# The norm behind w_o moved to scores and expert blocks, the residual turned raw, and decode's gelu put behind the next copy and split

## The reference

```python
x = x + mixed @ w_o
x = x + peer(rmsnorm(x, norm_ffn_g), peer_wq, keys1, keys2, u, v)

def rmsnorm(x, g):
    return x * rsqrt(mean(x * x, -1) + EPS) * g

def peer(x, wq, keys1, keys2, u, v):
    q  = (x @ wq)                       # 8 heads, 256 wide: two halves of 128
    s1 = q[..., :half] @ keys1.T        # scores; s2 likewise with keys2
    ...                                 # top 16 of each, top 16 of their sums, softmax -> gate
    z   = x @ u[expert]                 # inner products with the chosen experts
    act = gelu(z) * gate
    return act @ v[expert]
```

## Time and profile before

| | us |
|---|---|
| median of 3 runs | 2696.15 (2695.79 to 2697.1) |
| profiled execution | 2696.89 |
| its span | 2695.2 |
| PE busy | 2669.4 (99%) |
| DVE busy | 1835.3 (68%) |
| ACT busy | 1369.4 (51%) |
| POOL busy | 371.4 (14%) |

### The profile page before, as it was taken

One profiled execution on the slowest core, in us unless ns is written; L12 is line 12 of the kernel. 1 busy time (PEld: TensorE's weight loads), 2 busy tenths in 40 slices (PEclk: granted clock), 3 DMA queues, 4 the chain that ended last, 5 costly groups with the idle time before them and its releaser, 6 DMA issues.

```text
span 2695.2 us, 47112 instructions
## 1 busy us (share of the span) xinstructions
PE 2669.4 (99%) x14299; PEld 2298.4 (85%) x14299; DVE 1835.3 (68%) x2985; ACT 1369.4 (51%) x2066; POOL 371.4 (14%) x296
## 2 busy tenths in 40 slices
PE   8999999999999999999999999999999999999998
PEld 6888888898888998888888888888888888888887
DVE  6666665668987677489996777775565555555555
ACT  6454445555665444455455555554444444444444
POOL 0010000001011211011105555551000000000000
PEclk9999999999999999999999999999999999999999
DMA  7566555564554554655567777777976666666564
GB/s 257 189 216 213 181 199 177 177 219 159 172 176 156 167 168 157 195 201 186 195 201 212 202 202 203 201 204 218 305 240 217 217 217 219 212 220 216 200 241 156
DMA packets 204475, 543.26 MB, mean 202 GB/s; under 512 B 37504, under 2 KB 82816, under 8 KB 203392
## 3 DMA queue, kind: packets, MB, share of 16 engines
q1 hardware_dynamic: 148112, 486.74, 54.9%
q10 hardware_dynamic: 35568, 47.33, 5.0%
q0 software_dynamic: 20736, 8.46, 2.7%
HBM read 515.12 MB, written 27.33 MB: 201 GB/s over the span
## 4 chain that ended last, share of the span: by engine, by line
PE 94%; DVE 3%; ACT 1%; issue 1%; DMA 0%; SPq 0%; DVEq 0%; POOL 0%; ACTq 0%; POOLq 0%
PE bank L561 32%; PE bank L568 16%; PE bank L2693 8%; PE bank L2694 8%; PE bank L2695 8%; PE bank L601 4%; PE bank L603 4%; PE bank L602 4%; PE bank L2488 1%; DVE w_lo L504 1%; PE bank L527 1%; PE bank L528 1%; PE bank L529 1%; PE bank L2658 1%; PE bank L2465 0%
## 5 line engine op out<-in xcount | busy, mean ns | idle before, releaser
L504 DVE TENSOR_TENSOR w_lo<-raw,w_hi 128x1024 fp32r<-128x1024 f32 x902 | 1097.9, 1226 | 725.9 <-ACT w_hi L495 719.4
L495 ACT ACTIVATE w_hi<-raw 128x1024 fp32r<-128x1024 f32 x902 | 950.8, 1059 | 946.5 <-PE bank L568 363.1
L561 PE MATMUL bank<-act,w_hi 128*128 128x512 f32 x3840 | 975.2, 396 | 2.6 <-DVE cst L579 1.0
L561 PEld LDWEIGHTS bank<-act,w_hi 128*128 128x128 f32 x3840 | 692.0, 189 | 133.8 <-issue 6.4
L568 PEld LDWEIGHTS bank<-act,w_lo 128*128 128x128 f32 x3840 | 519.7, 190 | 33.1
L568 PE MATMUL bank<-act,w_lo 128*128 128x256 f32 x3840 | 535.6, 282 | 0.0
L2693 PE MATMUL bank<-w_hi,expert_act 128*128 128x512 f32 x1008 | 392.3, 389 | 0.1
L2694 PE MATMUL bank<-w_lo,expert_act 128*128 128x512 f32 x1008 | 392.2, 389 | 0.0
L2695 PE MATMUL bank<-w_hi,expert_act 128*128 128x512 f32 x1008 | 392.1, 389 | 0.0
L742 POOL DMA_INDIRECT g_kept<-slot_t x128 | 239.7, 1872 | 253.8 <-issue 170.4
L2693 PEld LDWEIGHTS bank<-w_hi,expert_act 128*128 128x128 f32 x1008 | 189.3, 188 | 39.6 <-DVE cst L579 0.5
(11 more groups left out here) (344 smaller groups left out, 2498.4 us busy)
## 6 DMA issues: line engine op xcount, KB each, us to landing
raw<-in_stream SPq DMA_DIRECT2D x902, 512.0 KB
z_kept<-cst ACTq DMA_DIRECT2D x112, 128.0 KB, 2.4
cst<-z_kept ACTq DMA_DIRECT2D x112, 128.0 KB, 3.9
g_kept<-zeros POOLq DMA_DIRECT2D x16, 512.0 KB
big<-in_ukv ACTq DMA_DIRECT2D x16, 512.0 KB, 4.6
big<-g_kept SPq DMA_DIRECT2D x16, 512.0 KB, 5.6
big<-in_rows ACTq DMA_DIRECT2D x3, 1024.0 KB, 5.8
big<-in_x SPq DMA_DIRECT2D x2, 1024.0 KB, 10.2
```

Source lines behind the costliest of these rows:

```text
L495: act.activation(w_hi[:, s, :], raw[:, s, :], ACT.Copy).then_inc(hi_ready, 1)
L504: dve.tensor_tensor(w_lo[:, s, :], raw[:, s, :], w_hi[:, s, :].bitcast(F32), ALU.subtract).then_inc(lo_ready, 1)
L561: pe.matmul(bank[:, :], w_hi[:, s, kk * P:(kk + 1) * P], act2[:, k, :, :].rearrange("p a n -> p (a n)"), start=(k == 0), stop=False)
```

## The change

It does four things.

1. X is turned without the norm. `turn_block` (eight transposes of a quarter of X's columns for one half of the tokens) is called with the raw X: three of the four blocks between units of w_o, the fourth between the two units of the first query pair. The hi and lo tiles come from the helpers that the first block uses, `keep_hi_tiles` and `keep_lo_tiles`. XN and its eight pieces are gone.
2. The factor 1/root (`rstd`, one number a token) is put on products instead. ACT's copy of the scores takes it as its scale, in two copies of 128 columns where there was one of 256. For the expert blocks, whose columns are tokens, DVE builds two diagonal tiles, PE multiplies them with ones to a row that is the same in all partitions, and ACT copies that row to `FFN_ROW`.
3. Each expert block is multiplied with `FFN_ROW` ahead of its gelu: the router's early blocks by POOL (`early_block`), the 16 decode blocks by POOL in a loop that stands ahead of the scatter, the 80 gates and 16 late blocks by DVE (`scale_rows`). ACT's gelu waits for `z_scaled` where it waited for the add.
4. In decode ACT's turn is now: split of unit 0, copy of block k, split of unit 1, and then gelu and store of block k-1.

```diff
+            def early_block(n, block):
+                z = Z_HALVES[:, n, 0:S]
+                pool.wait_ge(copied, block + 5)
+                step(pool.tensor_tensor(z, z, Z_HALVES[:, n, S:2 * S], ALU.add))
+                pool.wait_ge(row_kept, 2)
+                step.wait()
+                pool.tensor_tensor(z, z, FFN_ROW, ALU.mult).then_inc(pool_summed, 1)
...
+            with pool.Fori(0, PH) as i:
+                for n in range(2):
+                    wait_summed(pool, block_of("u_decode", i, 2, n))
+                    pool.tensor_tensor(GZ[:, n, :], GZ[:, n, :], FFN_ROW, ALU.mult).then_inc(z_scaled, 1)
             pool.wait_ge(picks_ready, 5)
...
+                        else:
+                            keep_hi_tiles(3, pa("ffn_gain"), act_hi, k // 4 - 1)
                         block_squares(added, base, k // 4 - 1)
...
-                if not t:
-                    ahead(split_hi, act, "w_o", 0, 8, 15, units=(0,))
-            act.wait_ge(rstd_ready, 7)
-            norm_second(2)
-            keep_ffn_hi(range(4))
-            norm_second(3)
-            keep_ffn_hi(range(4, 8))
+            ahead(split_hi, act, "w_o", 0, 8, 15, units=(0,))
+            keep_hi_tiles(3, pa("ffn_gain"), act_hi, 3)
             ahead(split_hi, act, "w_o", 0, 8, 15, units=(1,))
-            keep_ffn_hi(range(8, 16))
...
-                    act.activation(PS[:, a, :, :].rearrange("p t n -> p (t n)"), banks[4 + a][:, 0:S],
-                                   ACT.Copy).then_inc(ps_kept[a], 1)
+                    for t in range(TT):
+                        kept = act.activation(PS[:, a, t, :], banks[4 + a][:, t * P:(t + 1) * P], ACT.Copy,
+                                              scale=rstd[:, t:t + 1])
+                    kept.then_inc(ps_kept[a], 1)
...
+                if first:
+                    act.wait_ge(row_made, 2)
+                    act.activation(FFN_ROW, banks[6][:, 0:S], ACT.Copy).then_inc(row_kept, 1)
+                    act.wait_ge(rstd_ready, 7)
                 keep_scores(0)
...
                     ahead(split_hi, act, "u_decode", i, 2, n, units=(0,))
+                    act.wait_ge(unit_done, 2 * pair_of("u_decode", i, 2, n) + 2)
+                    act.wait_ge(z_saved[n], i * 16 + (16 * PH + 1))
+                    low_half(act, GZ[:, n, :], banks[2 + n])
+                    ahead(split_hi, act, "u_decode", i, 2, n, units=(1,))
                     if first and not n:
                         save_early(PH - 1, 1, 4 * PH - 1)
                     else:
                         save_decoded(i, n - 1)
-                    act.wait_ge(unit_done, 2 * pair_of("u_decode", i, 2, n) + 2)
-                    act.wait_ge(z_saved[n], i * 16 + (16 * PH + 1))
-                    low_half(act, GZ[:, n, :], banks[2 + n])
-                    ahead(split_hi, act, "u_decode", i, 2, n, units=(1,))
...
             def save_decoded(i, n):
-                wait_summed(act, block_of("u_decode", i, 2, n))
+                act.wait_ge(z_scaled, i * 2 + (n + 1))
...
+                        if part == "w_o" and b and k == 1:
+                            keep_lo_tiles(4, pa("ffn_gain"), act_hi, act_lo, b - 1)
...
-            dve.wait_ge(added[1], 8)
-            norm_last(0, 0)
             add_last(1)
-            for cc in range(1, 4):
-                norm_last(0, cc)
             mean_last(1)
             root_last(1)
-            dve.wait_ge(added[1], 9)
-            norm_last(1, 0)
-            norm_last(1, 1)
-            keep_ffn_lo(range(8))
             ahead(split_lo, dve, "w_o", 0, 8, 15, units=(0,))
-            keep_ffn_lo(range(8, 16))
+            keep_lo_tiles(4, pa("ffn_gain"), act_hi, act_lo, 3)
+            step(dve.memset(ONES, 1.0))
+            for t in range(TT):
+                step(dve.tensor_scalar(RSTD_DIAG[:, t, :], ident, rstd[:, t:t + 1], None, ALU.mult))
+            step.wait()
+            dve.sem_inc(rstd_ready, 1)
             ahead(split_lo, dve, "w_o", 0, 8, 15, units=(1,))
...
+            def scale_rows(n, block):
+                wait_summed(dve, block)
+                dve.tensor_tensor(GZ[:, n, :], GZ[:, n, :], FFN_ROW, ALU.mult).then_inc(z_scaled, 1)
...
                     add_gates(i, n)
+                    scale_rows(n, block_of("u_gates", i, 2, n))
...
-            mix_block(1, 1, range(6))
+            mix_block(1, 1, range(4))
+            turn_block(2, 2, added, 4)
+            mix_block(1, 1, range(4, 6))
...
+            def first_queries():
+                pe.wait_ge(copied, 1)
+                pe.wait_ge(added[1], 8)
+                pe.wait_ge(act_lo_ready, 4 * KT + 12)
+                halves_out(pe, pair_of("wqu", 0, 4, 0), odd_of("wqu", 0), banks[0], units=(0,))
+                turn_block(2, 3, added, 4)
+                halves_out(pe, pair_of("wqu", 0, 4, 0), odd_of("wqu", 0), banks[0], units=(1,), paced=4 * KT)
...
+            first_queries()
             queries_out(0, 1)
+            pe.wait_ge(rstd_ready, 8)
+            for t in range(TT):
+                ins = pe.matmul(banks[6][:, t * P:(t + 1) * P], ONES, RSTD_DIAG[:, t, :], start=True, stop=True)
+            ins.then_inc(row_made, 1)
```

More of the change, by code:

```diff
@@ L729, in add_copied @@
                 pool.tensor_tensor(dest, halves[:, 0:S], halves[:, S:2 * S], ALU.add).then_inc(pool_summed, 1)
-            with pool.Fori(0, PH) as h:
-                for a in range(2):
-                    pool.wait_ge(ps_made[a], h + 1)
-                    add_copied(PQS[:, a, :], QUERY_HALVES[:, a, :], h * 4 + a)
+            def early_block(n, block):
[5 more added lines that the diff above has]
+                pool.tensor_tensor(z, z, FFN_ROW, ALU.mult).then_inc(pool_summed, 1)
+            with pool.Fori(0, PH) as h:
+                with step.turns(h, 2, PH):
+                    for a in range(2):
+                        pool.wait_ge(ps_made[a], h + 1)
+                        add_copied(PQS[:, a, :], QUERY_HALVES[:, a, :], h * 4 + a)
+                    for n in range(2):
+                        early_block(n, h * 4 + (2 + n))
+            with pool.Fori(0, PH) as i:
                 for n in range(2):
-                    add_copied(Z_HALVES[:, n, 0:S], Z_HALVES[:, n, :], h * 4 + (2 + n))
+                    wait_summed(pool, block_of("u_decode", i, 2, n))
+                    pool.tensor_tensor(GZ[:, n, :], GZ[:, n, :], FFN_ROW, ALU.mult).then_inc(z_scaled, 1)
             pool.wait_ge(picks_ready, 5)
@@ L1109, in _ @@
                 act.activation(std[:, t:t + 1], ss[:, t:t + 1], ACT.Sqrt).then_inc(std_ready, 1)
-                if not t:
-                    ahead(split_hi, act, "w_o", 0, 8, 15, units=(0,))
-            def norm_second(cc):
-                cols = slice(cc * 512, (cc + 1) * 512)
-                act.activation(XN[:, 1, cols], X[:, 1, cols], ACT.Copy, scale=rstd[:, 1:2]).then_inc(normed_s, 1)
-            def keep_ffn_hi(chunks):
-                gain = pa("ffn_gain")
-                for k in chunks:
-                    act.wait_ge(turned, 3 * KT + k // 2 * 2 + 2)
-                    act.activation(act_hi[:, k, :], ffn_chunk(k), ACT.Copy, scale=gain[:, k:k + 1])\
-                       .then_inc(act_hi_ready, 1)
-            act.wait_ge(rstd_ready, 7)
-            norm_second(2)
-            keep_ffn_hi(range(4))
-            norm_second(3)
-            keep_ffn_hi(range(4, 8))
+            ahead(split_hi, act, "w_o", 0, 8, 15, units=(0,))
+            keep_hi_tiles(3, pa("ffn_gain"), act_hi, 3)
             ahead(split_hi, act, "w_o", 0, 8, 15, units=(1,))
-            keep_ffn_hi(range(8, 16))
             act.dma_start(KEYT, keys_t).then_inc(table_ready, 16)
@@ L1949, in root_last @@
                 dve.wait_ge(rstd_ready, 6 + t)
-            def norm_last(t, cc):
-                cols = slice(cc * 512, (cc + 1) * 512)
-                dve.tensor_scalar(XN[:, t, cols], X[:, t, cols], rstd[:, t:t + 1], None, ALU.mult).then_inc(normed, 1)
-            def keep_ffn_lo(chunks):
-                gain = pa("ffn_gain")
-                for k in chunks:
-                    dve.wait_ge(act_hi_ready, 4 * KT + k // 2 * 2 + 2)
-                    dve.scalar_tensor_tensor(out=act_lo[:, k, :], in0=ffn_chunk(k), scalar=gain[:, k:k + 1],
-                                             in1=act_hi[:, k, :].bitcast(F32), op0=ALU.mult, op1=ALU.subtract)\
-                       .then_inc(act_lo_ready, 1)
             dve.wait_ge(added[0], 9)
@@ L2247, in turn_rows, with turn_block @@
                 pe.wait_ge(act_lo_ready, fill * KT + 10)
-            def turn_block(turn, b, taken):
-                pe.wait_ge(taken[b % 2], b // 2 * 2 + 3)
+            def turn_block(turn, b, taken, base=0):
+                pe.wait_ge(taken[b % 2], base + b // 2 * 2 + 3)
                 if 4 * turn + b >= 2:
```

45 lines of the change are left out of this document (14 added, 31 removed).

## The result

The changed kernel takes 2702.84 us (median of 16 runs) against 2696.16 us (16 runs): ratio 1.0025, 95% interval 1.0018 to 1.0032. It is slower by 6.7 us, where +3.1 was forecast. One of its sixteen runs took 6896.65 us, lies far outside all others and stays unexplained; the others lie between 2698.92 and 2715.08.

What follows compares the result with a forecast made beforehand. PE was taken as the bound, busy 2669.4 of 2695.2 us. Terms -3.5 (transition), +1.8 (ACT's order) and +4.8 (POOL's product) sum to +3.1, forecasting 2699.3 us, range 2693.5 to 2703.5.

Steps and rivals of the forecast that it cites:

- Transition: From the last w_o matmul to the second query pair: 14.05 us of before shrinks, a gain of 3.5 us.
- wait in unit 1: First query pair: unit 1's later matmuls wait for the last four lo tiles, taken as 0.9 us.
- stall inside w_o: Sign that would prove the forecast wrong: raw blocks' tiles coming late inside w_o, costed at nothing.
- POOL's product: Decode: POOL's product and DVE's operations hold each other off, 0.54 us a block for nine blocks, +4.8 us.
- a whole pair to spare: Decode, ACT's new order: blocks other than the one before the first gates pair have this room, so no cost.
- The first rival: Decode: POOL's product slips in beside DVE at no price, sum -1.7, 2694.5 us; chance 0.20.
- Starving POOL: Decode: DVE leaves POOL no gap, factor a block late, PE waits over 1 us a block, 2706 or more; chance 0.08.
- Order on ACT: End of decode: first gates pair waits for block 14's gelu, 1.98 us once, about 0.2 back: +1.8 us.
- The store rival: Decode: ACT's copies wait for stores to land, about 3 to 4 us on top, 2703 us; chance 0.17.
- The scatter: POOL's 128 indirect DMAs start near 1444, end near 1870, before SP's load at 1881.9: no cost, margin about 10 us.
- Gates and late blocks: DVE's added product of about 0.42 us a block stays covered there: no cost; uncovered, up to 0.4 for each of 80 blocks.

Runs made afterwards that it cites:

- the product on tiles nobody reads: Changed kernel with POOL's decode product, same size and moment, on two tiles nobody reads; ACT's gelu waits for DVE's add alone: 2702.11 us.
- Moving one gelu: Changed kernel with the gelu of block 14 put ahead of block 15's copy, ACT's old order in the last decode block alone: 2698.74 us.
- memset run: Changed kernel with POOL's decode product replaced by a constant fill of a same-size tile; ACT's gelu waits for DVE's add alone: 2697.99 us.
- the run with both prices out: Changed kernel without POOL's product in decode and with the gelu of block 14 ahead of block 15's copy: 2696.64 us.
- early-scatter twin: Changed kernel without POOL's decode product or loop, so the scatter starts near 1413, and with block 14's gelu ahead of block 15's copy: 2695.27 us.
- late scatter: Version deferring the 16 decode blocks' factor and gelu to the second expert product (2693.4 us), with POOL's indirect DMAs waiting for the fourth gates block: 2704.42 us.

## Why the prediction was right or wrong

- **Transition, -3.5: right.** 7.50 us for 7.4, 0.45 for 0.5, -3.4 at the start of decode. The wait in unit 1 was 0.3 in its row and 1.15 by starts (1158.42 to 1162.37 for 2.80), where 0.9 was taken. No stall inside w_o.
- **POOL's product, +4.8: right in place, mechanism and price of a block; the match of the total is partly luck.** 0.53 to 0.55 a block in DVE's rows, pairs 6.55 apart for 6.5, decode 4.6 us longer in all. But without the product the profiled decode gives only 3.7 back, some seven blocks' worth where nine were counted. The 1.0 that is left is the new order's, for which the prediction had nothing ("a whole pair to spare"). The first rival (POOL slips in beside) falls: the product on tiles nobody reads costs the same. Starving POOL did not occur; its longest product is 2.72.
- **Order on ACT, +1.8: the term of the sum that was too small.** In the profile it measured 3.9 at the end of decode: a wait of 2.4 and a first gates pair longer by 1.5. Moving one gelu takes 4.1 off the median, 2.6 of which the profiles show there. Two things were missing in the term. The copy ahead of the gelu waited for the store of block 13 (1440.66 instead of 1440.2), which the prediction had as a rival of its own and did not let into this term. And TensorE ran at 1.2 GHz for 3.4 us behind the wait. The trace of before could not show that: from 10 us on PE stood still for at most 1.3 us at a stretch, at a granted clock of 1.00. Whether the clock falls is not settled by the wait's length, since behind the 2.62 us of the memset run it did not; how many of the changed kernel's other runs paid this 1.5 us is not known.
- **The store rival, 0.17: half right.** Copies did wait for stores, three in the changed kernel and eight without POOL's product, but PE had the room for most of them; its 3 to 4 us did not come. Without the product 0.9 to 1.4 us of it show in decode, which is part of why taking out both prices leaves 2695.3 and not 2693.4.
- **The scatter, nothing with a margin of 10 us: wrong in its size.** The start of 1444 was right. That the scatter always takes the 425 us of the one profiled execution was not: 419 to 440 us in the profiles here. In the changed kernel's profile it ends at 1866 and costs nothing; in other runs SP waits for it. That this makes the changed kernel's wide runs (2715.08) is inferred from the run with both prices out, its early-scatter twin and the late scatter, not seen in those runs themselves. Why the scatter's length varies stays open.
- **Gates and late blocks, nothing:** +0.3 us for all that is left, as far as the span tells.

The median lies inside the range, 0.7 us under its upper bound, and that is partly luck: the bound was built from DVE standing for all of POOL's product and half of the store rival, neither of which came. The forecast time missed by 3.5 us, 1.5 of it the clock, about 0.5 the store at the end; the median lies another 1.2 above what the two profiles differ by, which fits single runs held by the scatter, but isn't resolved.

## What to carry to other kernels

Work that is moved to an idle engine isn't free when it reads SBUF beside a full VectorE: look for rows where the two overlap, count the extension, and multiply by the blocks in the full stretch alone (here some seven of sixteen). Put the work where the bound engine's feeders have room (here a later product, where the same 16 factors and gelus cost nothing) rather than where an engine looks idle. And when a step moves a long DMA chain on one queue, follow it to the reader's wait on every other queue, with the spread of its length and not one value.

## What the runs showed of the hardware

- TensorE's clock fell to 1.2 GHz for 3.4 us at single waits of PE of 1.8, 2.0, 2.3 and 2.9 us, and for 10.2 us at one of 8.4; where it fell, a pair of 5.9 to 6.0 us took some 1.5 longer. It stayed at 2.4 GHz through a wait of 2.6 us in the memset run. Near 24 us of the program, at the same wait of 1.06 or 1.07 us, it fell in three profiles and stayed up in six. So the length of a wait alone did not tell; what did is not shown.
- A POOL product of 128x256 that reads SBUF took 0.74 alone and 1.12 to 2.72 beside DVE's two-input operations, and made the DVE operation behind it 0.53 to 0.55 longer. One operation with a single input was held too, a TENSOR_SCALAR of 128x256 uint32: 0.85 for 0.29. A POOL memset of the same tile held no two-input operation; beside a CAST the first of them took 0.50 for 0.31, and the CAST 0.62 for 0.42.
- 128 indirect DMAs from POOL took 419 to 440 us in the twelve profiles, from the first start to the last.
